# Scalar decays in the state branch, and a new order around the convolutions, in a two-block hybrid layer

## The reference, cut to what matters

```python
proj = h @ w_in
(m_z, m_xbc, m_dt, b_qkv, c_qkv, c_f, d_q, d_kv, gate_logits) = jnp.split(proj, SPLIT_POINTS, axis=-1)

# state branch (8 heads, one chunk of 256 tokens)
xbc = silu(causal_depthwise_conv(m_xbc, conv_w, conv_b))      # xs, bm, cm
dt = softplus(m_dt + dt_bias)
acum = cumsum(dt * (-exp(a_log)))                             # per head, over tokens
decay_in = exp(where(causal, acum[l] - acum[s], -inf))        # l: query token, s: key token
y = (cc @ bc.T * decay_in) @ (xs * dt) + d_skip * xs          # then gated by silu(m_z), rmsnorm

# forgetting attention (8 heads)
cum = cumsum(log_sigmoid(c_f + forget_bias))
s = q @ k.T * scale + (cum[query] - cum[key])
out = softmax(where(causal, s, -inf)) @ v

# two more attention branches, then
sum(sigmoid(gate_logits) * (branches @ w_branch)) @ w_out     # and a gated feed-forward layer
```

## Time and profile before

| | us |
|---|---|
| three executions | 940.95, 943.91, 942.98 |
| median | 942.98 |
| the profiled execution | 941.52 |
| its span, first to last instruction | 939.7 |
| TensorE busy in it | 924.0 |
| VectorE busy | 609.8 |
| ScalarE busy | 471.7 |
| GpSimd busy | 62.3 |

### The profile page before, as it was taken

One profiled execution on the slowest core, in us unless ns is written; L12 is line 12 of the kernel. 1 busy time (PEld: TensorE's weight loads), 2 busy tenths in 40 slices (PEclk: granted clock), 3 DMA queues, 4 the chain that ended last, 5 costly groups with the idle time before them and its releaser, 6 DMA issues.

```text
span 939.7 us, 16383 instructions
## 1 busy us (share of the span) xinstructions
PE 924.0 (98%) x6835; PEld 808.5 (86%) x6835; DVE 609.8 (65%) x973; ACT 471.7 (50%) x721; POOL 62.3 (7%) x79
## 2 busy tenths in 40 slices
PE   9999999999999999999999999999999999999998
PEld 8999987787778789999988789888887788888886
DVE  6785445557678766666653769578867568776344
ACT  5654335546774454444443674556436445554331
POOL 1000000020002300000000000002450000000000
PEclk9999999999999999999999999999999999999999
DMA  9995452234446544555553442222001345555521
GB/s 323 290 284 223 187 198 96 92 144 148 137 185 250 189 157 179 190 192 199 195 204 126 179 160 90 90 90 92 3 2 30 153 179 190 188 203 206 199 90 46
DMA packets 16874, 149.85 MB, mean 159 GB/s; under 512 B 1744, under 2 KB 6224, under 8 KB 8352
## 3 DMA queue, kind: packets, MB, share of 16 engines
q1 hardware_dynamic: 14688, 140.24, 40.0%
q0 software_dynamic: 1296, 5.24, 3.0%
q10 hardware_dynamic: 816, 3.31, 0.9%
HBM read 144.59 MB, written 4.19 MB: 158 GB/s over the span
## 4 chain that ended last, share of the span: by engine, by line
PE 84%; DVE 5%; ACT 4%; issue 2%; DMA 2%; POOL 1%; SPq 1%; DVEq 0%; ACTq 0%; POOLq 0%
PE bank L700 56%; PE bank L748 6%; PE bank L657 4%; PE bank L750 3%; PE bank L1520 3%; DMA weights<-weights_dram 2%; DVE W_LOW L2328 2%; PE bank L922 1%; ACT W_HIGH L1752 1%; POOL HN L3235 1%; PE bank L963 1%; PE bank L1000 1%; DVE ARENA L2375 1%; PE bank L1387 1%; PE bank L1281 0%
## 5 line engine op out<-in xcount | busy, mean ns | idle before, releaser
L2328 DVE TENSOR_TENSOR W_LOW<-weights,W_HIGH 128x2048 fp32r<-128x2048 f32 (+1 forms) x98 | 224.5, 2291 | 185.2 <-ACT W_HIGH L1752 185.1
L1752 ACT ACTIVATE W_HIGH<-weights 128x2048 fp32r<-128x2048 f32 (+1 forms) x98 | 186.7, 1906 | 222.3 <-PE bank L700 180.0
L700 PE MATMUL bank<-OVER_BOTH,W_HIGH 128*128 128x256 f32 x704 | 124.5, 280 | 0.1
L700 PEld LDWEIGHTS bank<-OVER_BOTH,W_HIGH 128*128 128x128 f32 x704 | 107.7, 188 | 0.4 <-DVE W_LOW L2328 0.3
L700 PE MATMUL bank<-OVER_BOTH,W_LOW 128*128 128x256 f32 x352 | 98.5, 280 | 0.0
L748 PE MATMUL bank<-OVER_BOTH,W_HIGH 128*128 128x512 f32 x256 | 89.1, 392 | 0.0
L700 PE MATMUL bank<-W_HIGH,HID_HIGH 128*128 128x512 f32 x200 | 77.9, 390 | 0.0
L700 PE MATMUL bank<-W_HIGH,HID_LOW 128*128 128x512 f32 x200 | 77.9, 389 | 0.0
L700 PE MATMUL bank<-W_LOW,HID_HIGH 128*128 128x512 f32 x200 | 77.8, 389 | 0.0
L750 PE MATMUL bank<-OVER_BOTH,W_LOW 128*128 128x256 f32 x256 | 71.6, 280 | 0.0
L700 PEld LDWEIGHTS bank<-OVER_BOTH,W_LOW 128*128 128x128 f32 x352 | 66.2, 188 | 0.0
(11 more groups left out here) (534 smaller groups left out, 1954.8 us busy)
## 6 DMA issues: line engine op xcount, KB each, us to landing
weights<-weights_dram SPq DMA_DIRECT2D x62, 2048.0 KB, 7.9
weights<-weights_dram SPq DMA_DIRECT2D x3, 1024.0 KB, 9.2
bias_rows_dram<-ARENA POOLq DMA_DIRECT2D x1, 3072.0 KB, 39.9
BIAS<-params_dram ACTq DMA_DIRECT2D x1, 1997.0 KB, 12.8
weights<-weights_dram SPq DMA_DIRECT2D x1, 1664.0 KB, 6.9
weights<-weights_dram SPq DMA_DIRECT2D x1, 1584.0 KB, 7.2
weights<-weights_dram SPq DMA_DIRECT2D x3, 512.0 KB, 5.6
X<-x_dram ACTq DMA_DIRECT2D x2, 512.0 KB, 4.3
```

The source lines that it names most:

```text
L700: ins = pe.matmul(o, left[a][k], right[b][k], start=(first and k == 0 and a + b == 0), stop=(last and k == n - 1 and a == 1))
L1752: act.activation(like_source(piece_parts(k)[0], k), piece_source(k), ACT.Copy).then_inc(sem("pieces_high"), 1)
L2328: dve.tensor_tensor(low, piece_source(k), high.bitcast(F32), ALU.subtract)\
```

## The change

- State scores: one matmul per unit writes the query's cumulated rate to all key rows; the key's rate comes as a scalar per partition (`KEY_RATES`, in columns that held convolution weights), added by VectorE together with the mask, in two instructions.
- Forgetting attention: the query's term is no longer added (softmax over a row does not see it).
- The rates are turned behind chunk 5, dt and the cumulated row together, in four transposes; the bank changes.
- Softplus and scans move behind the convolutions and the splits of pieces 9 and 10, on both engines; what reads them moves behind them.
- In state pairs `gate_low(2p + 1)` stands between the two biases.
- Constants, final norm row and positions are loaded ahead of chunk 4 (the fifth); VectorE's wait for the constants moves from the table to the scans.

```diff
-FILLS += [(("dt_T",), 5), (("xs_T", 0), 6), (("xs_T", 1), 7), (("cb", 0), 4), (("cb", 1), 5)]
+FILLS += [(("xs_T", 0), 6), (("xs_T", 1), 7), (("cb", 0), 4), (("cb", 1), 5), (("dt_T",), 4)]
...
-                if k == 2:
+                if k == 4:
                     sp.dma_start(CST[:, P:NC], consts[:, P:NC]).then_inc(sem("consts_in"), 16)
...
+        KEY_RATES = prm("conv_w", 0, TT * NH)
...
-                if i == 2:
-
-                    pe.wait_ge(sem("dt_ready"), 1)
-                    o = open_fill(("dt_T",))
-                    for tt in range(TT):
-                        ins = pe.matmul(o[:, tt * NH:(tt + 1) * NH], SM8[0:NH, tt * P:(tt + 1) * P],
-                                        ident[0:NH, 0:NH], start=True, stop=True)
-                    close_fill(ins)
...
             for i in range(5, 11):
                 (t_jobs_split if ("in1", i) in TOKEN_CHUNKS else f_jobs_split)("in1", i, *first)
+                if i == 5:
+
+                    pe.wait_ge(sem("rates_cumulated"), 1)
+                    o = open_fill(("dt_T",))
+                    for n, rows in enumerate((SPX[:, 0:S], ACUM)):
+                        for tt in range(TT):
+                            a = (2 * n + tt) * NH
+                            ins = pe.transpose(o[:, a:a + NH], rows[:, tt * P:(tt + 1) * P], ident[0:NH, 0:NH])
+                    close_fill(ins)
...
-                            pe.matmul(o[:, c0:c1], cum[:, q0:q0 + P], both_parts(h, n, 1), start=False, stop=False)
...
-                o, h, a = BK[4 + u % 2], ALL_UNITS[u][1], DECAY_PARTS[:, 0:S]
-                for (c0, c1, s0) in ((0, S, 0), (S, 384, P)):
-                    pe.matmul(o[:, c0:c1], both_parts(h, P, 1), a[:, s0:S], start=True, stop=False)
-                    ins = pe.matmul(o[:, c0:c1], a[:, s0:s0 + P], both_parts(h, c1 - c0, -1), start=False, stop=True)
-                ins.then_inc(sem("scores_written"), 1)
+                pe.matmul(BK[4 + u % 2][:, 0:S], both_parts(ALL_UNITS[u][1], P, 1), DECAY_PARTS[:, 0:S], start=True, stop=True)\
+                    .then_inc(sem("scores_written"), 1)
...
-            softplus_parts(0, SPT)
             convs(0, 8)
             split_high(9)
             take(("in1", 3, 0), flat(CQ1[:, 0:2, :]), 0.125)
             split_high(10)
+            softplus_parts(0, SPT)
...
-            dve.wait_ge(sem("consts_in"), 16)
             o = fill_arrived(dve, ("table",))
...
-            minus_abs(SPX, SPT)
             split_low(3)
             split_low(4)
+            convs(0, 8)
+            minus_abs(SPX, SPT)
+            split_low(9)
+            take(("in1", 3, 1), flat(CQ1[:, 2:4, :]), 0.125)
+            split_low(10)
             softplus(0, SPX, SPT, SPX)
+            dve.wait_ge(sem("consts_in"), 16)
             dve.wait_ge(sem("a_ready"), 1)
...
-            convs(0, 8)
-            o = fill_arrived(dve, ("dt_T",))
-            fill_out(dve.tensor_copy(DTT, o[:, 0:TT * NH]), ("dt_T",))
-            split_low(9)
+            split_low(11)
+            take(("in1", 4, 1), flat(CK1[:, 2:4, :]), 1.0)
+            dve.wait_ge(sem("rates_cumulated"), 1)
             rows = SM8[0:NH, 768:1280]
...
-            take(("in1", 3, 1), flat(CQ1[:, 2:4, :]), 0.125)
-            split_low(10)
+            split_low(12)
+            split_low(13)
+            take(("in1", 5, 1), CV1[:, 1, :], 1.0)
+            o = fill_arrived(dve, ("dt_T",))
+            dve.tensor_copy(DTT, o[:, 0:TT * NH])
+            fill_out(dve.tensor_scalar(KEY_RATES, o[:, TT * NH:2 * TT * NH], -1.0, None, ALU.mult), ("dt_T",))
...
-                    dve.tensor_tensor(s, o[:, 0:384], cst("ssd_mask"), ALU.add).then_inc(sem("scores_read"), 1)
+                    for tt, (c0, c1) in enumerate(((0, S), (S, 384))):
+                        ins = dve.scalar_tensor_tensor(out=s[:, c0:c1], in0=o[:, tt * P:S], scalar=KEY_RATES[:, tt * NH + h:tt * NH + h + 1],
+                                                       in1=cst("ssd_mask")[:, c0:c1], op0=ALU.add, op1=ALU.add)
+                    ins.then_inc(sem("scores_read"), 1)
...
-                bias_scores(2 * p + 1)
-                gate_low(2 * p + 1)
+                if UNITS[2 * p][0] == 0:
+                    gate_low(2 * p + 1)
+                    bias_scores(2 * p + 1)
+                else:
+                    bias_scores(2 * p + 1)
+                    gate_low(2 * p + 1)
```

More of the change, by code:

```diff
@@ L2430, in _ @@
             dve.sem_inc(sem("params_halved"), 1)
-            minus_abs(SPX, SPT)
             split_low(3)
             split_low(4)
+            convs(0, 8)
[3 more added lines that the diff above has]
+            split_low(10)
             softplus(0, SPX, SPT, SPX)
+            dve.wait_ge(sem("consts_in"), 16)
             dve.wait_ge(sem("a_ready"), 1)
-            dve.tensor_scalar(DECAY, SPX[:, 0:S], EALOG[0:NH, :], -1.0, ALU.mult, ALU.mult).then_inc(sem("dt_ready"), 1)
-            dve.wait_ge(sem("dt_ready"), 1)
+            link(dve.tensor_scalar(DECAY, SPX[:, 0:S], EALOG[0:NH, :], -1.0, ALU.mult, ALU.mult))
             dve.tensor_tensor_scan(ACUM, ones[0:NH, :], DECAY, 0.0, ALU.mult, ALU.add)
-            link(dve.tensor_tensor_scan(FCUM, ones[0:NH, :], SPX[:, S:2 * S], 0.0, ALU.mult, ALU.subtract))
-            convs(0, 8)
-            o = fill_arrived(dve, ("dt_T",))
-            fill_out(dve.tensor_copy(DTT, o[:, 0:TT * NH]), ("dt_T",))
-            split_low(9)
+            dve.tensor_tensor_scan(FCUM, ones[0:NH, :], SPX[:, S:2 * S], 0.0, ALU.mult, ALU.subtract)\
+                .then_inc(sem("rates_cumulated"), 1)
+            split_low(11)
+            take(("in1", 4, 1), flat(CK1[:, 2:4, :]), 1.0)
+            dve.wait_ge(sem("rates_cumulated"), 1)
             rows = SM8[0:NH, 768:1280]
@@ L2458, in _ @@
                          ("xs_T", tt))
-            split_low(11)
-            take(("in1", 4, 1), flat(CK1[:, 2:4, :]), 1.0)
-            for i, dst, scale in ((5, CV1[:, 1, :], 1.0), (6, flat(DQ1[:, 2:4, :]), 0.125), (7, flat(BQ1[:, 2:4, :]), 0.125),
+            for i, dst, scale in ((6, flat(DQ1[:, 2:4, :]), 0.125), (7, flat(BQ1[:, 2:4, :]), 0.125),
                                   (8, flat(BK1[:, 2:4, :]), 1.0), (9, BV1[:, 1, :], 1.0)):
```

## The result

The changed kernel takes **948.87 us** (median of four executions, 948.22 to 949.66); the kernel before takes 941.97 beside it (940.78 to 943.91). The ratio is **1.0071**, with a 95% interval of 1.0058 to 1.0084: slower by 0.7%. The forecast was 936.5. The profiled execution took 949.66 with a span of 947.9.

What follows compares the result with a forecast made beforehand. TensorE, busy 924.0 of 939.7 us, was taken to bound the kernel. Gains of 1.7 (softplus), 1.8 (forgetting attention) and 2.3 (state branch) sum to 5.8 us, giving 936.5, range 934.4 to 939.8.

Steps and rivals of the forecast that it cites:

- Constants, norm row, positions: SP's load queue: moving these loads from ahead of chunk 2 to ahead of chunk 4 costs 0.
- rival (c): SP's load queue runs dry before the constants and chunk 4; held twice, chunk 4 lands 15 us late: 952, chance 0.04.
- a wait for the transfer of chunk 4: TensorE in the first projection: such a wait would show the forecast wrong; no size given.
- The rule I leaned on: DMA queues: each engine serves its queues in turn, by packets, so an empty queue's loads cannot be held.
- Softplus: First projection: softplus moved behind the convolutions closes TensorE's gaps before pieces 5 and 6, gain 1.7 us, bounds 0.2 and 1.9.
- Forgetting attention: Four pairs: dropping the query term saves 8 heads x 2 blocks x 0.11 = 1.8 us, bounds 0.9 and 4.3.
- State branch: Four pairs: two score matmuls remain of eight, gain 0.58 a pair, 2.3 us in all, bounds 0.8 to 2.9.
- The two additions: VectorE in state pairs: two scalar additions replace one 384-wide addition, near 0.62 us, bounds 0.51 and 1.02.
- the order: State pairs: the gate's subtraction between the biases ends at t + 2.47, 0.67 early; cost 0.
- Rival (b): State pairs: GpSimd keeps the shared port for both products, 0.3 us in each of three pairs: 937.5, chance 0.14.
- Rival (a): First projection: the split loop stays the bound, gaps return at piece 6 or 9, 0.2 of 1.7 us kept: 938.0, chance 0.13.
- The rates' transposes: Moved from behind chunk 2 to behind chunk 5: cost taken as 0, bounds 0.3 us gained and 0.6 lost.

Runs made afterwards that it cites:

- chunk 4 alone: The changed kernel with its three loads (constants, norm row, positions) moved from ahead of chunk 4 to ahead of chunk 6: 936.37 us, ratio 0.9929 to the kernel before.

## Why the prediction was wrong, point by point

**Constants, norm row, positions: "Cost 0".** This step failed, with 12 to 14 us. It counted bytes ("the same bytes go before it, in another order") and not what stands in the queue when they come. The sentence of rival (c) that spoke against it, "even 4.2 us earlier the queue has work until 30", took a landing for the end of work: chunk 3 landed near 30, but from 28 on the queue had 2.1% of the engines' time. The loads, issued at 27.41, were too late to keep it going. What the runs showed in place of "cost 0": nothing moved until about 41.5, the constants and the norm row then took until 57.5, chunk 4 landed behind them at 65.1, and TensorE stood 11.6 us. The prediction had named a wait for the transfer of chunk 4 as a sign of being wrong.

**Rival (c) was the case**, at a chance of 0.04. Its place and its point of decision were right: it decided from a landing of some 62, and chunk 4 landed at 65.1. Its price was made of whole holds, 53.6 or 68. What came was one hold of about 12 us, then a term that I had not: the sharing by packets, in which small ones lose, so that 1.1 MB ahead of chunk 4 took 16 us where I had 4.2. That the sum came near the price of two holds is luck. The clock added 1.5 to 2 us that no part of the forecast had, though the rival spoke of a long idle stretch.

**The rule I leaned on.** From 42 us on the engines serve the two queues one packet each, as the Trainium skill, page "DMA: Bandwidth & Descriptors", section "Queues, rings and completion order", says. From 30 to 41 this did not come about: SP had issued loads, and its queue moved nothing. Whether the engines already had these loads to serve, no trace here shows; but the rule, as I used it, said that the case cannot come, and it came. The 22.4 us of before had shown as much, and I had written that they disagree with the rule; a chance of 0.04 did not follow from that.

**Softplus, 1.7 us:** right in size. Both waits are gone in the changed kernel, and putting it back costs 1.9 to 2.5 by the times and 1.6 by the traces.

**Forgetting attention, 1.8 us:** measured 1.80, as 16 steps of 0.11 give it.

**State branch, 2.3 us:** measured 2.65. The two products pass in 0.34 (186.63 to 186.97), where I took 0.38. Timelines of TensorE, GpSimd and VectorE in the first pair where GpSimd works, answering to the earlier trace rows:

```profile
194.04 0.50 PE L937 MATMUL bank<-DECAY_PARTS,PICK_PARTS 128*128 128x256 f32 x2
```

```profile
194.30 2.98 POOL L3231 TENSOR_TENSOR ARENA<-ARENA 128x384 f32<-128x384 f32 x2 [134.76 <-PE bank L998]
```

```profile
194.47 0.74 DVE L2493 SCALAR_TENSOR_TENSOR ARENA<-bank,PRM,CST 128x256 f32<-128x256 f32 x2 [0.76 <-PE bank L937]
195.12 1.27 DVE L2475 TENSOR_TENSOR RING_LOW<-weights,GATE_HIGH 128x1024 fp32r<-128x1024 f32 x1
196.32 0.73 DVE L2493 SCALAR_TENSOR_TENSOR ARENA<-bank,PRM,CST 128x256 f32<-128x256 f32 x2
```

The two additions take 0.74 together, between my bounds of 0.51 and 1.02. The subtraction ends at 196.39, t + 2.35 (forecast t + 2.47). So the order, costed at nothing because the low half would come early, was costed rightly. What the forecast did not see is that the products need it: with the old order they bring 1.2 us, not 2.3.

**Rival (b)** did not come: VectorE got in between GpSimd's two products, and GpSimd paid, 2.98 us for two products against 1.98, and no wait of TensorE came of it. **Rival (a)** did not come either: with the loads back ahead of chunk 2, where no long wait covers it, TensorE has no wait from 20 to 150 us.

**The rates' transposes, cost 0:** 0.54 us where they stand now, 0.61 less where they stood.

## What to carry to other kernels

Before moving a load to a later place, ask what its queue holds at that moment and which other queue is busy: bytes that cost nothing in a full queue can be held for as long as another queue's bulk transfer lets them. A large store that nobody waits for is best kept away from the stretch in which the loads are just in time, and a load that is first read hundreds of us later need not stand there at all. Where two engines' chains are nearly equal, price an edit for the pair: removed products and the new order were worth 2.7 us together, the products alone 1.2 and the order alone nothing.

## What the runs showed of the hardware that was not expected

- A queue that runs dry while GpSimd's store has packets waiting got nothing, or next to nothing, for 11 to 15 us, whether constants or a chunk came next: 29.5 to 41.5 (the change, and chunk 4 alone), 41 to 55.5 (before), 41.5 to 52.5 (loads ahead of chunk 2). In the second run of that last kernel a few packets went through (0.56 MB from 42 to 52), and chunk 5 landed after 22.9 us all the same, against 22.6. Why it is that long stays open.
- With the engines to itself the store had 98% of their time and moved 97 GB/s, at 0.74 us a packet; beside a chunk's packets its own took 0.18 us.
- Right behind the held constants SP's next issues took 4.47 to 4.57 us, where the same issues take 0.43 to 0.48 without the store; an issue 11.5 us behind a held chunk took 0.33. The hold is not the only cause of a long issue: one took 2.58 us near 8 us, with no store yet.
- After 11.6 us without work TensorE's granted clock was 0.50, and 18 steps ran at 0.21 us; filling the idle time with products that nobody reads made the kernel 2.7 us faster.
